# Fillers taken out of the routing and the first expert round, put into the last one; earlier first reload, earlier transposes, a shared final norm

## The reference, cut to what is computed

```python
for layer in range(2):
    h = rmsnorm(x, norm_mix[layer])
    x = x + (even_mixer, odd_mixer)[layer](h, ...)   # attention heads / chunked gated linear attention
    h = rmsnorm(x, norm_ffn[layer])
    # MoE: 4 groups x 8 experts, best group, best 2 experts of it
    for e in range(32):
        hid = silu(h @ w_gate[e]) * (h @ w_up[e])     # 1024 -> 512
        y = y + gates[..., e:e+1] * (hid @ w_down[e]) # 512 -> 1024
    x = x + y
return rmsnorm(x, norm_final)
```

## Time and profile before

| what | value |
|---|---|
| median of 3 runs | 1184.88 us |
| the profiled execution: time / span | 1186.47 us / 1184.7 us |
| PE busy | 998.1 us, 84% |
| DVE, ACT busy | 276.8 us, 130.1 us |
| mean granted TensorE clock | 0.932 of full |
| data moved | 442.43 MB, mean 373 GB/s |
| chain that ended last | PE 52%, DMA 42%, issue 3% |

### The profile page before, as it was taken

How to read it: one execution, slowest core, us unless ns; L and a number is a source line. 1 busy time by engine, 2 the same in 40 slices (tenths; PEclk the granted TensorE clock), 3 DMA queues, 4 the chain that set the end, 5 groups by cost and what they waited for, 6 DMA issues and landing times.

```text
span 1184.7 us, 12720 instructions
## 1 busy us (share of the span) xinstructions
PE 998.1 (84%) x5268; PEld 457.9 (39%) x5268; DVE 276.8 (23%) x653; ACT 130.1 (11%) x309; POOL 3.5 (0%) x10
## 2 busy tenths in 40 slices
PE   8999999967767768977999999999677777779776
PEld 7675553313213213342485555533132132233422
DVE  1265352202102101110322453512011011012103
ACT  2024020000000000000231120200000000000001
POOL 0000000000000000000000000000000000000000
PEclk9999999989879879988999999999898798799889
DMA  9923989999999999999973518999999999999996
GB/s 365 411 77 133 418 329 425 428 427 428 427 430 427 428 429 427 426 426 423 412 327 142 213 71 340 352 428 426 426 430 427 428 429 426 429 427 428 425 422 249
DMA packets 39297, 442.43 MB, mean 373 GB/s; under 512 B 4386, under 2 KB 4770, under 8 KB 12484
## 3 DMA queue, kind: packets, MB, share of 16 engines
q1 hardware_dynamic: 39092, 441.47, 89.4%
q10 hardware_dynamic: 144, 0.13, 0.0%
HBM read 440.54 MB, written 1.05 MB: 373 GB/s over the span
## 4 chain that ended last, share of the span: by engine, by line
PE 52%; DMA 42%; issue 3%; DVE 1%; SPq 1%; ACT 0%; POOL 0%; DVEq 0%; POOLq 0%
PE psum L1707 51%; DMA sb_weights<-moe_w_down 38%; DMA sb_weights<-moe_w_gate 3%; SPq L668 1%; DMA sb_weights<-moe_w_up 1%; DMA sb_weights<-ev_w_in_units 1%; PE psum L2302 0%; DVE sb_weights L1578 0%; DVE sb_x L1598 0%; PE psum L1885 0%; PE psum L1745 0%; PE psum L2170 0%; PE psum L2080 0%; PE psum L1983 0%; ACT sb_weights L914 0%
## 5 line engine op out<-in xcount | busy, mean ns | idle before, releaser
L1707 PE MATMUL psum<-sb_weights,sb_hT 128*32 128x512 f32 (+3 forms) x2368 | 469.4, 629 | 102.9 <-DMA sb_weights<-moe_w_gate 59.8
L1707 PE MATMUL psum<-sb_weights 128*32 128x512 f32 (+12 forms) x1632 | 319.8, 561 | 43.5 <-DMA sb_weights<-moe_w_down 38.7
L1707 PEld LDWEIGHTS psum<-sb_weights,sb_hT 128*32 128x32 f32 (+2 forms) x2368 | 148.2, 128 | 396.0 <-issue 315.7
L1707 PEld LDWEIGHTS psum<-sb_weights 128*32 128x32 f32 (+7 forms) x1632 | 116.2, 139 | 235.2 <-issue 192.1
L1591 DVE TENSOR_TENSOR sb_x<-sb_x,psum 128x512 f32<-128x512 f32 x84 | 57.7, 687 | 281.6 <-PE psum L1707 281.6
L1707 PE MATMUL psum<-sb_hT,sb_weights 128*128 128x256 f32 (+1 forms) x400 | 88.8, 380 | 0.9 <-DMA sb_weights<-ev_w_in_units 0.8
L1707 PEld LDWEIGHTS psum<-sb_hT,sb_weights 128*128 128x128 f32 (+1 forms) x400 | 74.0, 187 | 13.5 <-issue 1.6
L1707 PE MATMUL psum<-sb_weights,sb_hn 128*128 128x192 f32 (+2 forms) x448 | 72.2, 321 | 6.4 <-issue 6.2
L1707 PEld LDWEIGHTS psum<-sb_weights,sb_hn 128*128 128x128 f32 x448 | 69.3, 204 | 11.1 <-issue 11.1
L1583 DVE COPY sb_weights<-psum 96x512 f32<-96x512 f32 (+1 forms) x20 | 13.7, 687 | 180.6 <-PE psum L1707 180.6
L1578 DVE TENSOR_TENSOR sb_weights<-sb_weights,psum 96x512 f32<-96x512 f32 (+1 forms) x22 | 15.0, 684 | 159.5 <-PE psum L1707 159.4
(11 more groups left out here) (201 smaller groups left out, 340.7 us busy)
## 6 DMA issues: line engine op xcount, KB each, us to landing
sb_weights<-moe_w_gate SPq DMA_DIRECT2D x60, 2048.0 KB, 24.5
sb_weights<-moe_w_down SPq DMA_DIRECT2D x58, 2048.0 KB, 27.1
sb_weights<-moe_w_up SPq DMA_DIRECT2D x50, 2048.0 KB, 27.1
sb_weights<-moe_w_up SPq DMA_DIRECT2D x18, 1024.0 KB, 23.2
sb_weights<-od_w_in_units SPq DMA_DIRECT2D x6, 2048.0 KB, 27.4
sb_weights<-ev_w_in_units SPq DMA_DIRECT2D x5, 2048.0 KB, 25.5
sb_weights<-moe_w_up SPq DMA_DIRECT2D x20, 512.0 KB, 8.5
sb_weights<-moe_w_gate SPq DMA_DIRECT2D x16, 512.0 KB, 7.1
```

Of the source, the lines that this page charges most:

```text
L1707: return nc.tensor.matmul(o, l, r, start=start, stop=stop, skip_group_check=True)
```

## The change

It has these parts:

1. `route` loses its two fillers (512 and 192 columns) and `expand_first`'s follower loses its filler of 384. The second token tile's logits and quarter transposes go ahead of the rank multiplies on PE, and `residual` on DVE does `turned_quarter(1)` and `inverse_root(n, 1)` ahead of `ranked` and the one-hot.
2. "Eighths": the first gate reload of the second round is split in two. The first half (256 KB for each of two experts) is issued as soon as row block j = 0 is multiplied, the second after j = 1.
3. The last round's scatter of the round before stands in front of `expand("gate")`, followed by two fillers of 512 columns; four more fillers of 512 columns stand between the transposes of the hidden values and the down multiply.
4. `project_out` calls its hook one block earlier (4 to 3 in layer 0, 6 to 5 in layer 1), and the last projection of `mixer1` is cut in two around `chunk_kv(3, 1)`.
5. The final norm: DVE multiplies the first half of the columns by the gain ahead of time (`final_gain`); after the root ACT scales that half and stores it from its own queue, DVE does the other half, and SP stores it.

```diff
@@ second_round (SP)
+                sp.wait_ge(quarter_used, 4 * layer + 1)
+                for k in range(1, LIGHT):
+                    src = A["moe_w_gate"][layer, LIGHT + k].rearrange("(p j) n -> p (j n)", p=P)
+                    sp.dma_start(unit[SLOT["gate"] + k][:, 0:HALF], src[:, 0:HALF]).then_inc(held_full, 16)
...
+                        begin = HALF if part == 0 and kind == "gate" else part * 2 * HALF
+                        rows = slice(begin, (part + 1) * 2 * HALF)
+                        if part < 3 and kind == "gate":
+                            sp.wait_ge(used, 4 * layer + part + 2)
@@ end of SP
-                for half in range(2):
...
+                sp.wait_ge(x_done, t + 1)
+                sp.dma_start(out[0, t * P:(t + 1) * P, HALF:D], y[:, t, HALF:D]).then_inc(out_stored, 16)
@@ end of ACT
             square_sums(4)
+            for t in range(TILES):
+                i = TILES * 4 + t
+                act.wait_ge(inv_done, i + 1 - TILES * 2)
+                nc.scalar.activation(y[:, t, 0:HALF], y[:, t, 0:HALF], ACT.Copy, scale=rrms[:, i:i + 1]
+                                     ).then_inc(late_scaled, 1)
+            for t in range(TILES):
+                act.wait_ge(late_scaled, 2 + t + 1)
+                act.dma_start(out[0, t * P:(t + 1) * P, 0:HALF], y[:, t, 0:HALF]).then_inc(out_stored, 16)
@@ DVE, residual
                 add_quarter(1)
+                turned_quarter(1)
+                inverse_root(n, 1)
                 ranked(layer, 0)
...
-                turned_quarter(1)
-                inverse_root(n, 1)
@@ DVE, final_rounds
-                add_round(s, r + 1, (0, 1))
+                if layer:
+                    dve.wait_ge(gfin_done, 2)
+                for t in range(TILES):
+                    add_round(s, r + 1, (t,))
+                    if layer:
+                        dve.wait_ge(s.x_added, (r + 1) * 4 + t + 5)
+                        final_gain(t)
@@ PE, mixers
-                            4, turn_mix)
+                            3, turn_mix)
...
-                project1(11, 1)
+                project1(11, 1, 0)
                 chunk_kv(3, 1)
+                project1(11, 1, 1)
...
-                            6, lambda: turn_o1(C_HEADS - 1))
+                            5, lambda: turn_o1(C_HEADS - 1))
@@ PE, route
+                logits(layer, 1, 0)
+                turn_quarter(layer, 1)
                 pe.wait_ge(mask_done, TILES * layer + 1)
...
-                logits(layer, 1, 0)
-                turn_quarter(layer, 1)
...
-                keep_warm(HALF, bank=1)
-
                 pe.wait_ge(mask_done, TILES * layer + 2)
...
-                keep_warm(192, bank=1)
@@ PE, expand_first
+                                if j == 0 and kind == "gate" and frees:
+                                    ins.then_inc(quarter_used, 1)
@@ PE, expert_round
+                if columns:
+                    scatter(s, n - 1, 1 - h, 0)
+                    scatter(s, n - 1, 1 - h, 1)
+                    keep_warm(HALF, HALF, bank=4)
...
-                if prior:
+                if prior and not columns:
...
-                if first:
-                    keep_warm(384, bank=5)
-                else:
+                if not first:
                     expand("up", 1)
...
+                if columns:
+                    keep_warm(HALF, HALF, HALF, HALF, bank=3)
                 pe.wait_ge(s.hidT_done, n + 1)
```

More of the change, by code:

```diff
@@ L1697, in _ @@
                     gains(1)
-            dve.wait_ge(gfin_done, 2)
             for t in range(TILES):
-                inverse(4, t)
+                mean_square(4, t)
+            for t in range(TILES):
+                inverse_root(4, t)
                 final_norm(t)
@@ L1784, in column_tokens, with project @@
                 return hTc[:, j, i * P:(i + 1) * P]
-            def project(layer, c, i, group, step, by_token, free=None):
+            def project(layer, c, i, group, step, by_token, free=None, part=None):
                 if c == layer == i == 0:
@@ L1806, in project @@
                                  j == 0, j == KT - 1)
-                if step == 1:
+                if step == 1 and part != 0:
                     ins.then_inc(proj_psum, 1)
@@ L1961, in project1 @@
                         free = (sg_done, g - 9)
-                    project(1, c, g % 2, g, step, None if c in COL_UNITS[1] else plain_tokens, free)
+                    project(1, c, g % 2, g, step, None if c in COL_UNITS[1] else plain_tokens, free, part)
                 def gates(c):
```

28 lines of the change are left out of this document (13 added, 15 removed).

## The result

| | median | runs | lowest to highest |
|---|---|---|---|
| before | 1185.16 us | 14 | 1184.13 to 1186.45 |
| changed | 1187.55 us | 14 | 1185.33 to 1191.49 |

The ratio is 1.0020, 95% interval 1.0013 to 1.0028. The forecast was 1181.0, its range ended at 1184.0, and "slower" had 0.05. The changed kernel also spreads over 6.2 us, where the kernel before spreads over 2.3.

The account below looks back on a forecast made before the run. Each layer was taken as a PE-bound mixer and routing, a gapless 192 MB weight stream at 427 GB/s, and a tail. Terms -1.6 + 0.2 - 1.9 + 0.3 + 0.5 - 1.4 = -3.9 gave 1181.0 us from 1184.88; range 1177.3 to 1184.0.

Parts of the forecast that it names:

- Term 1: Start of layer 0's weight stream: fillers removed, earlier hook and eighths start it sooner; -1.6 us (ends -2.1 and 0).
- Gate multiplies then start at 157.97 - 2.0: Layer 0's first round: with 2.0 us saved, gate multiplies start at 156.0 instead of 157.97.
- I take 1.4 of the 2.1: Layer 0's routing: of two fillers' 2.1 us on PE, 1.4 counted as saved, since DVE's ranks lie beside part.
- first rounds run cold: Rival, slower: both layers' first rounds at half clock, 10 us cold each; sum +5.1, 1190.0 us; chance 0.05.
- Term 2: Layer 0's last round: warm gate and earlier down against idle PE ahead of up's second half; +0.2 us.
- Term 5: Layer 1's last round: gain at best 0.3, slow clock after idle costs more; +0.5 us (ends -0.3 and +2.2).
- Term 3: Layer 1's mixer: waits of 0.9 and 0.8 us filled, and loads come earlier; -1.9 us (ends -1.0 and -2.0).
- Term 4: Start of layer 1's stream beyond the mixer's shift: eighths gain 0.4, slow clock may cost; +0.3 (ends -0.4 and +1.5).
- Term 6: Final norm and stores: work split over DVE and ACT, two store queues; -1.4 us (ends -0.9 and -1.8).
- gives back 0.4: The end: ACT's second store, last behind its two scales of 0.6 us, loses 0.4 us of the gain.

Follow-up runs that it names:

- e3: Kernel before with only the mixers' edits (hooks a block earlier, last projection split): 1183.35 us, -1.8 against before, ratio 0.9991.
- e15: Second run of the e7 kernel (routing's two fillers given up, logits ahead of the ranks): 1186.82 us, +1.8 against before, ratio 1.0013.
- e7: Kernel before with only the routing's two fillers given up and its order changed; first round's filler of 384 stays: 1186.80 us, +1.4, ratio 1.0015.
- e8: Changed kernel with the last rounds of the kernel before: 1185.52 us, +0.2 against before, ratio 0.9997.
- e9: Changed kernel without the four fillers ahead of down in the last rounds: 1185.37 us, 0.0 against before, ratio 0.9999.
- e14: The e13 kernel with the routing's two fillers cut to 192 and 128 columns: 1182.33 us, -2.7 against before, ratio 0.9978.
- e6: Kernel before with only the first round's filler of 384 columns given up: 1184.65 us, -0.7, ratio 0.9995.
- e1: Kernel before with only the last-round part (early scatters, two fillers behind them, four ahead of down): 1189.16 us, +4.0, ratio 1.0040.
- e4: Kernel before with only the final norm changed (halves on DVE and ACT, four stores over two queues): 1185.13 us, 0.0, ratio 0.9998.
- e11: Kernel before with only the routing's order changed, all fillers kept: 1185.05 us, -0.3 against before, ratio 0.9999.
- e13: Changed kernel with the old last rounds and all three fillers of routing and first round put back: 1182.07 us, -2.9, ratio 0.9979.
- e10: Kernel before with only the four fillers ahead of down in the last rounds: 1189.06 us, +3.7 against before, ratio 1.0039.
- e16: Second run of the e3 kernel (mixers' edits alone): 1183.88 us, -1.1 against before, ratio 0.9996.
- e2: Kernel before with only the routing changed: its two fillers and the first round's 384 gone, logits ahead of ranks: 1187.85 us, +2.7, ratio 1.0023.

## Why the prediction was wrong

The segments are differences of the marks' table, averaged over the traces that share the part.

**Term 1, the start of layer 0's stream: -1.6 forecast, about 0 measured.** The times inside it came true to 0.1 us (gate at 156.0, first eighth at 157.1, `up` at 158.5), and that was luck, since kernels with all the fillers start gate at these times too. What failed is the base. "Gate multiplies then start at 157.97 - 2.0" took the earlier trace rows for the kernel's usual course, but that execution had a cold spell in the gathers ahead of the fillers and in the first of them (0.57 in the earlier trace rows; the 16 gathers took 3.21 us where the changed kernel's took 2.00, the filler of 512 took 1.53). In nine of the ten other traces with the full fillers it took 1.05 us, gate began between 154.8 and 156.8, and `up`'s landing near 158 to 159 was the bound already. The fillers stood largely in DVE's waits: taking them out laid 0.66 + 0.51 = 1.17 us of wait bare, so "I take 1.4 of the 2.1" was too much as well, and what was left could not pass `up`. From `up`'s issue to down's issue it is 36.1 us in twelve traces with the routing's fillers and 36.8 in six without. The eighths gave nothing that can be told. The earlier hook did give its 0.6: counted from the issue of `up` of expert 2 in the mixer, `up` of expert 1 is issued 36.1 to 36.2 us later in all eight traces with it and 36.8 in all ten without (the first row is of the kernel before, the second of e3):

```profile
111.95 0.33 SPq L586 DMA_DIRECT2D sb_weights<-moe_w_up  x1
...
112.72 0.33 SPq L586 DMA_DIRECT2D sb_weights<-moe_w_up  x1
```

Nothing of it can be seen at down's issue: that is 72.3 to 72.8 us behind the same mark in the five traces with the earlier hook and the fillers, and 72.2 to 72.5 in the five with the fillers, the old hook and no cold spell. So with -0.7 and +0.7 the term is 0; without e15, whose `up` landed late, the +0.7 is +0.1.

**The rival "first rounds run cold" names something that happens, at the wrong size.** It was priced at 10 us of cold clock in each layer and given 0.05. What happens is one short spell at 0.50, in some executions and not in others. In traces without the routing's fillers it is there in 5 of 12 first rounds (e7 twice, e8, e9, e15): the first 24 multiplies of `expand_first` took 5.1 to 5.5 us instead of 3.6 to 4.0. With the fillers (the short ones of e14 counted in) it is there in 4 of 24 (before and e6 in layer 0, e1 and e4 in layer 1), but in the 96-column gathers and the fillers ahead of `expand_first`, never in it. So the fillers don't abolish the spell, and 5 of 12 beside 4 of 24 is too few to show that they make it rarer. Nor does a spell cost 1.6 us: from `up`'s issue to down's, e7, e8 and e9 have 36.5 to 36.6 us in layer 0 where the two traces with neither fillers nor a spell have 35.7 and 35.8; with fillers and a spell it is 36.8, where e4 has 35.6. That is some 0.8 us in the one case and 1.3 in the other.

Part of the loss comes out only later. From `up`'s issue to the last adds, with the old last round, the four traces without the routing's fillers have 436.5 us in layer 0 and 436.0 in layer 1, the ten with them 435.7 and 435.3. Together that is 1.5 us, the size that e7 and e15 measured (1.4 and 1.8), but it rests on few traces: most of it is e15's late `up` in layer 0 and e7 in layer 1. So the loss is shown by times (e7, e15 against e11; e13 against e8), and how the fillers prevent it is shown in part only. The argument against this rival, that "the parts are dense 512-column multiplies", failed: such multiplies did run cold, behind a sparse stretch. The prediction's reason for the cold window, that the multiplies there have 32 to 96 columns, doesn't decide it either, since in 20 of the 24 places with fillers the same multiplies ran at 1.00. The Trainium skill's rule (TensorE: Matmul & The Clock Gate, "HAM oscillation"), cited in the prediction, speaks of bursts behind waits for loads; here it holds behind five of six waits of 3.8 us for a load, and behind the routing's waits for DVE, of 0.66 and 0.51 us, which are not its case, in under half of them.

**Term 2, layer 0's last round: +0.2 forecast, +2.6 measured.** From down's issue in the first round to the last adds, 14 traces with the old last round have 398.9 to 400.2 us (e10's, with four fillers in it, not counted), 399.4 in the mean; the changed kernel has 401.53 and e1 402.47. Three steps failed. "Down starts at 575.1 at full clock" left out that up's second half would be cold, though the term's own upper bound had it: 1.7 us, and it came in all three traces with the early up in this layer (5.33, 5.33 and 6.19 us). And "the load has 1.0 us to spare, and no more can be gained here" again took a cold execution (12.75 us) as the base. In ten of the 14 (e4, e8, e13 and e14 among them) down took 11.7 to 11.8 us with 0.2 to 0.4 us of wait for its last load, and in e3, e15 and e16 11.1 to 11.2 with none. So the old order stands at the edge of being bound by the load: it can start down up to 0.4 us later for nothing, and all beyond that is lost. Against this the term laid four fillers of 3.63 us, of which ACT's copy hides 0.58. They are the larger step: e10, with nothing else changed and nothing cold in its down, has 401.66 us here and 400.87 in layer 1, so 2.2 and 1.3 us more than the old last rounds, of the 3.7 that its times lost. The cold half costs less than it takes: counted from down's issue, the transposes of the hidden values start after 387.6, 388.6 and 388.8 us in the changed kernel, e1 and e9, and after 386.4 to 387.9 with the old order, and the times of e9 and e8 are level.

**Term 5, layer 1's last round: +0.5 forecast, +0.8 in the mean of two traces** (from down's issue to the last adds, 399.6 in 14 traces, 401.11 in the changed kernel and 399.65 in e1). Mechanism and size lie inside the term's range, and the two traces tell the clock's share apart. In the changed kernel up's second half was cold (5.33 us behind 3.82 of idle), and layer 1 is late by 1.5 us. In e1 the clock stayed up behind the same wait (first row below), down began right behind the fillers, and nothing was lost in this segment:

```profile
1159.90 3.63 PE L1707 MATMUL psum<-sb_weights,sb_hT 128*32 128x512 f32 x24 [3.83 <-DMA sb_weights<-moe_w_up]
1164.96 3.63 PE L1707 MATMUL psum<-sb_lead 128*128 128x512 f32 x8
```

**Term 3, the mixer: -1.9 forecast, -1.6 to -1.9 measured.** From layer 0's last adds to down's issue in layer 1, eight traces with the edits have 189.4 us, ten without 191.3. The part up to the issue of `up` of expert 1 hardly varies: 153.6 us in all eight, 155.2 in all ten, so -1.6, the two waits and no more (first row before, second e3):

```profile
740.97 0.33 SPq L586 DMA_DIRECT2D sb_weights<-moe_w_up  x1
...
737.75 0.33 SPq L586 DMA_DIRECT2D sb_weights<-moe_w_up  x1
```

No wait of 0.9 and 0.8 is left. e3 and e16 are 1.8 and 1.1 us faster; the interval of neither excludes that nothing changed, while those of e13 and e14, which have the edits too, do.

**Term 4: +0.3 forecast, about 0 measured.** From layer 0's last adds to down's issue in layer 1, the three traces without the routing's fillers and with the old mixer (e2, e7, e15) have 191.1 us, the seven with fillers 191.3; what the missing fillers cost behind down's issue is counted above.

**Term 6, the end: -1.4 forecast, -0.7 measured** (8.36 us from the last adds to the end in six traces with it, 9.07 in twelve without). "The last SP issue starts about 1.8 us earlier" came true: SP is through with its issues 5.0 us behind the start of the last adds (1180.00 + 1.21 - 1176.20), not 6.9 (1179.38 + 3.14 - 1175.63). What was mis-sized is "gives back 0.4": from there to the end of the span it is 3.4 us instead of 2.2, with four stores issued within 1.2 us on two queues. The times of e4 alone (0.0) don't show the gain; its interval allows it.

**The sum.** The segments give -0.7 + 0.7 + 2.6 - 1.9 + 0.8 - 0.7 = +0.8 us; the times say +2.4 (1.5 to 3.3). The 1.6 us between stay open: each trace is one execution, the clock's spells differ from one to the next, and the last rounds' terms rest on two traces, one of them 1.2 us below its kernel's median. The four parts and the eighths alone sum to 4.0 + 2.7 - 1.8 + 0.0 - 0.1 = +4.8, also more than the whole; their intervals of some 1 us each leave that undecided. What is shown without them is the direction: without the last rounds the loss goes (e8), without the four fillers too (e9), and with the fillers kept as well as the old last rounds it turns into a gain (e13, e14). So two terms failed: term 1 took 1.4 us from removing fillers that stood in waits, where the runs show nothing gained there and a loss of 1.4 to 1.8 in all, and term 2 laid four fillers ahead of down at no cost, where the runs show 3.7 us for both layers.

## What to carry to other kernels

Fillers belong in a wait that another engine or a load ends: 192 and 128 columns in waits of 0.66 and 0.51 us were as good as 512 and 192, while four of 512, some 2 to 3 us longer than the wait they stood in and ahead of a load-bound tail, cost 3.7 us. Before a row is taken as the base of a sum, see in which clock it was taken: one profiled execution with cold spells in two stretches made two edits look worth 1.4 and 1.0 us that gained nothing. An idle time moved from ahead of gate to behind it moved the cold multiplies too, from gate (8.4 to 10.0 us in all old last rounds but one, instead of 7.07) to up's second half (5.3 to 6.2 instead of 3.6); by the times the two orders came out level. To price an edit of a stretch, cut the traces at marks close around it: the mixers' two gains repeat to 0.02 us there, where medians are good to about 1.

## What the runs showed of the hardware that was not expected

The clock can fall in the middle of dense multiplies, not only at a wait. In e7 it was 1.00 through the two half-idle windows and the first dense one, and then 0.61 and 0.50 (rows above). And it can fall with no wait ahead at all: in the kernel before, PE was busy throughout the gathers of 96 columns when it went from 1.00 to 0.50:

```profile
151.46 3.21 PE L1707 MATMUL psum<-sb_weights,sb_hn 128*128 128x96 f32 x16
```

```profile
151.00:152.00 1.00, 1.00 (x9) 1.00 (x10) 0.26 (x2) 0.96 (x1) 0.00 (x0) 1.00 1.01 410
152.00:153.00 1.00, 1.00 (x8) 1.00 (x6) 0.84 (x5) 1.00 (x1) 0.00 (x0) 0.50 1.10 467
```

A load can be late with DMA nearly idle. In e15 `up` of expert 1, issued at 147.81, landed at 159.66 (the start of the multiply that waits for it), after 11.8 us, where it was 9.8 in the changed kernel and 10.2 in e3; the windows around its landing:

```profile
156.00:157.00 1.00, 0.99 (x9) 0.08 (x3) 0.00 (x0) 0.00 (x0) 0.00 (x0) 1.00 0.12 49
157.00:158.00 1.00, 0.00 (x0) 0.00 (x0) 0.00 (x0) 0.00 (x0) 0.00 (x0) 1.00 0.09 20
158.00:159.00 1.00, 0.00 (x0) 0.00 (x0) 0.00 (x0) 0.00 (x0) 0.00 (x0) 1.00 0.81 217
159.00:160.00 1.00, 0.34 (x3) 0.15 (x6) 0.00 (x0) 0.00 (x0) 0.00 (x0) 0.91 0.77 221
```

Two windows with 49 and 20 GB/s passed while the load was outstanding; what held it was not found.
